# A two-block transformer kernel: gate and up products of 20 tile pairs per FFN layer by a seven-product scheme, with the weight sums as GpSimd additions

## The chip, the core and the metric

The kernel runs on one core of one Trainium2 chip. The metric is the device time of one execution in microseconds (us), lower is better; a median of several runs is compared. Engines are named TensorE (PE, its weight loads PEld), VectorE (DVE), ScalarE (ACT), GpSimd (POOL) and SyncE (SP, which issues the weight loads).

## What is computed

Two models in a row on one sequence of 512 tokens, 1024 wide, all float32: an attention block, then two layers that each end in a gated FFN. The change concerns this function, once per layer, with `D_FF = 2816`:

```python
def gated_conv_ffn(x, w_gate, w_up, conv_w, conv_b, w_down):
    g = jnp.einsum('bsd,df->bsf', x, w_gate)
    g = causal_dwconv3(g, conv_w) + conv_b
    up = jnp.einsum('bsd,df->bsf', x, w_up)
    return jnp.einsum('bsf,fd->bsd', jax.nn.silu(g) * up, w_down)
```

`x` is `rms_norm(h, norm_ffn)`. `causal_dwconv3` is a convolution over the sequence with three taps per channel.

## The kernel before

Every product is made of 128x128 tiles of weights (stationary) and 512 columns of activations (moving), with channels on partitions and tokens in the free dimension. To reach float32 accuracy each operand is split into a high part (a cast to fp32r) and a low part (value less high part), and each tile product is three matmuls (`PASSES`: high-high, high-low, low-high). A unit is one 128-wide output tile of a weight matrix: 8 tiles over the 1024 inputs, 512 KB. SyncE loads a unit into one of two buffers `raw` (`w_load`, two DMAs), ScalarE casts it into one of two buffers `wsp` (`w_hi`, L305), VectorE subtracts (`w_lo`, L321), TensorE runs 24 matmuls (`product`, L364). GpSimd does the low part in other phases (L319). The order on each engine is written out by hand; semaphores that count finished steps are the only link between engines, and each engine works its own queue strictly in order.

In an FFN layer the 2816 hidden channels are 22 tiles, and each tile `f` has a gate unit and an up unit (a tile pair). `pe_ffn` runs them two tiles at a time over banks 0 to 3 of PSUM. `dve_ffn` scales the gate result with the token norm `rbc` (L2441), adds two of the three taps (L2446), multiplies with up (L2456) and makes the low part of the result (L2461); `act_ffn` does the first tap (L2407), SiLU (L2410) and the high part (L2416); `pool_ffn` scales SiLU's result with the norm (L2425). The results `a_r` are the moving operand of the down products (`pe_residual`, units of 8, 8 and 6 tiles, one output tile after the other), which follow at once. `rms_norm`'s factor is made while TensorE does the first FFN products: the sum of squares by a matmul (L1928), root on ScalarE (L1962), reciprocal on VectorE (L1970). It is applied to the products, so the products themselves run on unnormalised activations `u`.

The very last down tile (`pe_last_tile`) is done in halves of 256 columns (L1773). In the odd layer GpSimd multiplies with the gate (L2641) and VectorE makes low parts of what it made (L2645).

## Time and profile before

| | |
|---|---|
| median of 3 runs | 1754.58 us (1753.5 to 1755.64) |
| span of the profiled execution | 1753.3 us |
| TensorE busy | 1722.9 us, 98% |
| its weight loads busy | 1438.5 us, 82% |
| VectorE busy | 955.8 us, 55% |
| ScalarE busy | 776.2 us, 44% |
| GpSimd busy | 406.6 us, 23% |
| read from HBM | 147.02 MB, 85 GB/s |

The device time holds the span and what lies around it. Busy time is the union of an engine's instructions. Matmuls are pipelined: one of 512 columns lasts about 0.39 us from start to end, but the next starts long before that, so the time that a matmul costs is read from a run of them. An instruction's idle time is put down to the engine that released it. The column of a line's name such as L321 is the line in the kernel above.

### The profile page before, as it was taken

To read this page: it belongs to the slowest core of one execution; us is meant where nothing else is said; L and a number is where in the kernel's file an instruction comes from. 1 tells how busy PE (TensorE), PEld (TensorE's weight loads), DVE (VectorE), ACT (ScalarE), POOL (GpSimd) and SP (SyncE) were. 2 spreads that over 40 slices of the span, in tenths; PEclk is the share of its full clock that TensorE was granted. 3 is DMA by queue.
4 is the path that set the end of the run, shared out by engine and by line. 5 is a ranking of instruction groups with operands and counts; after the bars stand their busy time and mean duration, and the time that the engine had idled before them with its cause. 6 is when DMAs were issued, how large, how long until landed. Compare 5 with 4: busy or idle time off the path is not lost.

```text
span 1753.3 us, 25674 instructions
## 1 busy us (share of the span) xinstructions
PE 1722.9 (98%) x8611; PEld 1438.5 (82%) x8611; DVE 955.8 (55%) x1757; ACT 776.2 (44%) x1375; POOL 406.6 (23%) x545
## 2 busy tenths in 40 slices
PE   7999999999999999999999999999999999999998
PEld 7788889999878888888888888888788788888887
DVE  5677867777763334675555555333346555555332
ACT  6666766666652223432443333322364433333222
POOL 4555665655520001000211111011003211111000
PEclk9999999999999999999999999999999999999999
DMA  4112123333323334223233333333232333333332
GB/s 137 52 45 63 42 59 79 81 74 87 75 67 96 96 108 133 61 85 101 84 108 93 94 93 95 120 95 94 96 96 72 87 94 96 96 96 93 93 96 91
DMA packets 284314, 154.42 MB, mean 88 GB/s; under 512 B 12655, under 2 KB 278770, under 8 KB 284242
## 3 DMA queue, kind: packets, MB, share of 16 engines
q1 hardware_dynamic: 281714, 148.69, 29.4%
q0 software_dynamic: 2336, 4.47, 1.1%
q8 instruction: 42, 0.69, 0.2%
q10 hardware_dynamic: 192, 0.33, 0.1%
q14 instruction: 30, 0.25, 0.0%
HBM read 147.02 MB, written 2.16 MB: 85 GB/s over the span
## 4 chain that ended last, share of the span: by engine, by line
PE 82%; DVE 8%; issue 4%; ACT 4%; POOL 1%; DMA 0%; ACTq 0%; DVEq 0%; SPq 0%; POOLq 0%
PE ps L364 65%; PE ps L980 3%; PE ps L2505 2%; PE ps L830 2%; DVE tmp L1323 1%; DVE arena_r L1328 1%; PE ps L843 1%; PE ps L809 1%; ACT tmp L1051 1%; PE ps L788 1%; PE ps L1773 1%; ACT w_split L305 1%; PE ps L347 1%; PE ps L676 1%; DVE tmp L1380 1%
## 5 line engine op out<-in xcount | busy, mean ns | idle before, releaser
L364 PE MATMUL ps<-u,w_split 128*128 128x512 f32 x3705 | 876.9, 394 | 0.0
L364 PEld LDWEIGHTS ps<-u,w_split 128*128 128x128 f32 x3705 | 690.8, 188 | 152.1 <-issue 1.4
L321 DVE TENSOR_TENSOR w_split<-w_raw,w_split 128x1024 fp32r<-128x1024 f32 (+1 forms) x221 | 268.2, 1214 | 434.3 <-ACT w_split L305 434.2
L305 ACT CAST w_split<-w_raw 128x1024 fp32r<-128x1024 f32 (+4 forms) x321 | 289.0, 914 | 412.3 <-PE ps L364 376.6
L364 PE MATMUL ps<-arena_r,w_split 128*128 128x512 f32 x1758 | 402.0, 389 | 1.8 <-POOL w_split L319 1.5
L364 PEld LDWEIGHTS ps<-arena_r,w_split 128*128 128x128 f32 x1758 | 329.5, 188 | 72.2 <-POOL w_split L319 1.9
L2425 POOL TENSOR_TENSOR tmp<-tmp 128x512 f32<-128x512 f32 x44 | 57.1, 1298 | 422.1 <-ACT tmp L2410 422.1
L319 POOL TENSOR_TENSOR w_split<-w_raw,w_split 128x256 fp32r<-128x256 f32 x168 | 122.9, 763 | 23.7 <-ACT w_split L305 23.7
L980 PE MATMUL ps<-u,w_split 128*128 128x264 f32 x768 | 105.8, 287 | 2.0 <-DVE arena_r L1348 1.8
L1921 POOL TENSOR_TENSOR tmp<-tmp 128x512 f32<-128x512 f32 x33 | 46.8, 1417 | 261.1 <-ACT tmp L1877 232.4
L1051 ACT ACTIVATE tmp<-ps,stats 128x144 f32<-128x144 f32 (+3 forms) x128 | 69.4, 542 | 75.1 <-DVE stats L1315 73.0
L980 PEld LDWEIGHTS ps<-u,w_split 128*128 128x128 f32 x768 | 98.6, 188 | 4.6 <-DVE arena_r L1348 2.6
L1918 POOL COPY tmp<-tmp 128x512 f32<-128x512 f32 x5 | 3.2, 649 | 332.3 <-ACT tmp L1877 166.7
L1549 POOL TENSOR_TENSOR tmp<-tmp,ones 128x48 f32<-128x48 f32 x128 | 44.9, 351 | 151.1 <-DVE tmp L1323 151.0
L1315 DVE CUSTOM_DVE_ANT_0 ps<-ps,tmp 128x144 f32<-128x144 f32 (+3 forms) x128 | 65.6, 513 | 23.6 <-issue 22.1
L2410 ACT ACTIVATE tmp<-tmp,vec 128x512 f32<-128x512 f32 x44 | 31.9, 724 | 97.2 <-DVE tmp L2446 97.2
L1067 ACT CAST arena_r<-ps 128x128 fp32r<-128x128 f32 (+3 forms) x128 | 54.6, 426 | 35.1 <-PE ps L809 34.0
L1323 DVE TENSOR_SCALAR tmp<-tmp,stats 128x144 f32<-128x144 f32 (+3 forms) x128 | 66.5, 520 | 4.5
L2446 DVE SCALAR_TENSOR_TENSOR tmp<-tmp,vec 128x512 f32<-128x512 f32 x88 | 65.9, 749 | 5.5 <-DVE tmp L2446 0.3
L2416 ACT CAST arena_r<-tmp 128x512 f32 (+1 forms) x44 | 27.3, 620 | 87.2 <-DVE tmp L2456 87.2
L1328 DVE TENSOR_TENSOR arena_r<-ps,arena_r 128x128 fp32r<-128x128 f32 (+3 forms) x128 | 62.3, 487 | 3.7 <-ACT arena_r L1067 2.2
L809 PE MATMUL ps<-cst,tmp 128*128 128x128 f32 x320 | 57.1, 276 | 3.6 <-DVE arena_r L1328 3.2
(283 smaller groups left out, 1701.1 us busy)
## 6 DMA issues: line engine op xcount, KB each, us to landing
w_raw<-in_w_in_dram SPq DMA_DIRECT2D x118, 256.0 KB, 3.1
w_raw<-in_w_ffn_gate_dram SPq DMA_DIRECT2D x88, 256.0 KB, 3.1
w_raw<-in_w_ffn_up_dram SPq DMA_DIRECT2D x88, 256.0 KB, 3.2
w_raw<-in_w_ffn_down_dram SPq DMA_DIRECT2D x64, 256.0 KB, 3.1
w_raw<-in_w_in_even_dram SPq DMA_DIRECT2D x32, 256.0 KB, 3.0
w_raw<-in_w_in_odd_dram SPq DMA_DIRECT2D x32, 256.0 KB, 3.1
w_raw<-in_w_ffn_down_dram SPq DMA_DIRECT2D x32, 192.0 KB, 2.7
w_raw<-in_w_br_mla_dram SPq DMA_DIRECT2D x16, 256.0 KB, 3.1
```

The costliest lines, as they stand in the source:

```text
L305: ins = act.copy(dst, src)
L319: ins = eng.tensor_tensor(lo[:, at_:at_ + n], r[:, at_:at_ + n], hi[:, at_:at_ + n], ALU.subtract)
L321: ins = eng.tensor_tensor(lo, r, hi, ALU.subtract)
L364: last = pe.matmul(out_ap, w_tile(c, ws, k - n0), moving(k, ms), start=start and n == 0, stop=stop and n == len(total) - 1, skip_group_che ...
L809: ins = pe.transpose(bank(p_bank(b), j * P, (j + 1) * P), prob[:, b % 2, META + j * P:META + (j + 1) * P], ident)
L980: ins = pe.matmul(bank(b, 0, HALF), w_tile(c + j, ws, k), u[:, k, ms, half * HALF:(half + 1) * HALF], start=k == 0 and n == 0, stop=k == K ...
L1051: act.activation(probs(b), scored(b), ACT.Exp, bias=neg[:, b:b + 1], scale=-1.0, accum_out=rs[:, b:b + 1]) \
L1315: dve.tensor_tensor_reduce(out=scored(b), in0=scored(b), in1=mask, scale=1.0, scalar=3.0e38, op0=ALU.add, op1=ALU.min, accum_out=neg[:, b: ...
L1323: dve.tensor_scalar(p, p, ri[:, b:b + 1], None, ALU.mult).then_inc(sem("normed"), 1)
L1328: dve.tensor_tensor(lo, src, hi, ALU.subtract).then_inc(sem("p_split"), 1)
L2425: pool.tensor_tensor(cnv[:, j, :], cnv[:, j, :], rbc[:, 0, :], ALU.mult) \
L2446: dve.scalar_tensor_tensor(out=cnv[:, j, :], in0=gpad[:, j, tap:tap + SEQ], scalar=ffn_vec(layer, tap, f), in1=cnv[:, j, :], op0=ALU.mult, ...
```

## The change

Seen from one tile pair, gate and up are a 2 x 2 block product: two output tiles (gate, up) and two halves of the 1024 inputs on the weight side, and two halves of the inputs and two halves of the 512 tokens on the activation side. Eight block products, in Winograd's form, become seven products `p1` to `p7` of sums of blocks. Each is 4 tiles x 3 passes = 12 matmuls of 256 columns. The first two pairs of each layer (`PLAIN = 2`) stay as they were; 20 pairs use the scheme.

- Weights: a pair is loaded in quarters g1, g2, u1, u2 (the input halves of gate and up, 512 columns wide each, 256 KB). GpSimd makes four sums per pair, in place except the first: e = u1 + u2, u1 += g1, g1 += e, g2 += g1. The seven stationary operands are u1 + g1, g1, g1 + e, e, u2, g2 and g2 + g1. ScalarE casts each (`act_seventh`, L2599 of the changed kernel) and VectorE subtracts (`seventh_low`, L2605), into four slots, three products ahead of TensorE.
- Activations: they must be normalised now, since sums over tokens are formed. VectorE writes `x_tok` (8 instructions, L2636), GpSimd makes four sums 1024 wide (`pool_x`), and ScalarE and VectorE split seven operands `xs` (`act_x`, `dve_x`), once per layer.
- Results: p1 and p6, then p7 and p4 accumulate in one PSUM bank per tile; ScalarE copies it away in between (`snap` 1, 2, 3, L2691), and VectorE adds the right halves and the left half (`add_up_right` L2860, `add_gate_left` L2867, `add_gate_right` L2873). p4 and p3 of a pair are done after p1 of the next pair, the order is p1, p4, p3 (of the pair before), p2, p6, p5, p7. Then the taps (L2697, L2822), SiLU (L2702), product (L2879), high part (L2707) and low part (L2885).
- GpSimd's scaling of SiLU's result is left for the two plain pairs only.
- Semaphores of the prologue are merged, buffers are moved or laid over one another, and the load of `w_spatial` in the odd layer waits for the FFN's last low part.

```diff
+PLAIN = 2
+HT = SEQ // 2
+QUARTER = 4 * P
...
+SEVEN = ("p1", "p4", "p3", "p2", "p6", "p5", "p7")
+OF_LAST = (1, 2)
+ORDER = ([(PLAIN, p) for p in (0, 3, 4, 5, 6)] + [(f, p) for f in range(PLAIN + 1, FT) for p in range(7)]
+         + [(FT, p) for p in OF_LAST])
...
+WEIGHT_OF = {"p1": "g1", "p2": "g2", "p3": "g2", "p4": "u2", "p5": "e", "p6": "g1", "p7": "u1"}
...
-    phase(("ffn", 0), *("full",) * (2 * FT))
+    phase(("ffn", 0), *("full",) * (2 * PLAIN))
...
+            for name in ("u1", "u2", "g1", "g2"):
+                if not first:
+                    if name == "u1":
+                        low_split(sp, layer, i, gs - 2, 6)
+                    elif name != "g2":
+                        low_split(sp, layer, i, gs - 1, 1 if name == "u2" else 2)
...
+            if kind == "p1":
+                out_ = bank(R_BANK + gs % 2, 0, HT)
+                if not (isinstance(i, int) and gs < PLAIN + 2):
+                    pe.wait_ge(sem("ffn_a_done"), per_tile(layer, i, gs, 2))
+            elif kind == "p2":
+                out_ = bank(T_BANK, 0, HT)
+                if not (isinstance(i, int) and gs == PLAIN):
+                    pe.wait_ge(sem("combined"), combined(layer, i, gs - 1, "gate_left"))
+            elif kind == "p5":
+                out_ = bank(Q_BANK, 0, HT)
+                if not (isinstance(i, int) and gs == PLAIN):
+                    pe.wait_ge(sem("combined"), combined(layer, i, gs - 1, "gate_right"))
+            elif kind in ("p4", "p3"):
+                out_ = bank(R_BANK + gs % 2, 0, HT) if kind == "p4" else bank(Q_BANK, 0, HT)
+                pe.wait_ge(sem("combined"), combined(layer, i, gs, "up_right"))
+            else:
+                out_ = bank(R_BANK + gs % 2, 0, HT)
+                pe.wait_ge(sem("snap"), snapped(layer, i, gs, {"p6": 1, "p7": 2}[kind]))
+            for kk in range(4):
+                for n, (ws, ms) in enumerate(PASSES):
+                    ins = pe.matmul(out_, split_slot(layer, fs, pos, ws)[:, kk * P:(kk + 1) * P], XS[kind][:, kk, ms, :],
+                                    start=kind in ("p1", "p2", "p5") and kk == 0 and n == 0, stop=kk == 3 and n == 2,
...
+            act.copy(split_slot(layer, fs, pos, HI), quarter(layer, gs, WEIGHT_OF[kind])).then_inc(sem("s_hi"), 1)
...
+        def seventh_low(eng, layer, i, fs, pos):
+
+            eng.wait_ge(sem("s_hi"), used(layer, i, fs, pos))
+            src = quarter(layer, pair_of(fs, pos), WEIGHT_OF[SEVEN[pos]])
+            eng.tensor_tensor(split_slot(layer, fs, pos, LO), src, split_slot(layer, fs, pos, HI), ALU.subtract) \
+                .then_inc(sem("s_lo_pool" if pos in POOL_LO else "s_lo"), 1)
...
+        def pool_x(pool, layer, m):
+
+            pool.wait_ge(sem("x_dve"), X_STEPS * layer + KT)
+            if m in (1, 3):
+                pool.wait_ge(sem("x_sum"), 4 * layer + m)
+            dst, in0, in1, op = ((T1N, B11, B12, ALU.subtract), (T2, T1N, B22, ALU.add), (T3, B22, B12, ALU.subtract),
+                                 (T4, T2, B21, ALU.subtract))[m]
+            pool.tensor_tensor(dst, in0, in1, op).then_inc(sem("x_sum"), 1)
...
+            def first_sum(i, gs):
+                loaded(pool, layer, i, gs)
+                if not (isinstance(i, int) and gs < PLAIN + 2):
+                    low_split(pool, layer, i, gs - 2, 5)
+                    pool.wait_ge(sem("summed_w"), summed_to(layer, i, gs - 2, 2))
...
+                pool.tensor_tensor(quarter(layer, gs, "e"), quarter(layer, gs, "u1"), quarter(layer, gs, "u2"), ALU.add) \
+                    .then_inc(sem("summed_w"), 1)
...
+            def third_sum(i, gs):
+                pool.wait_ge(sem("summed_w"), summed_to(layer, i, gs, 1))
+                dst = quarter(layer, gs, "u1")
+                pool.tensor_tensor(dst, dst, quarter(layer, gs, "g1"), ALU.add).then_inc(sem("summed_w"), 1)
...
+            def second_sum(i, gs):
+                low_split(pool, layer, i, gs, 0)
+                pool.wait_ge(sem("summed_w"), summed_to(layer, i, gs, 3))
+                dst = quarter(layer, gs, "g1")
+                pool.tensor_tensor(dst, dst, quarter(layer, gs, "e"), ALU.add).then_inc(sem("summed_w"), 1)
...
+            def fourth_sum(i, gs):
+                low_split(pool, layer, i, gs, 3)
+                pool.wait_ge(sem("summed_w"), summed_to(layer, i, gs, 2))
+                dst = quarter(layer, gs, "g2")
+                pool.tensor_tensor(dst, dst, quarter(layer, gs, "g1"), ALU.add).then_inc(sem("summed_w"), 1)
...
+            def period(i, fs):
+                if fs == FT:
+                    return
+                fourth_sum(i, fs)
+                if fs < FT - 1:
+                    first_sum(i, fs + 1)
+                    third_sum(i, fs + 1)
+                    second_sum(i, fs + 1)
+
...
+            plain_gate(0)
+            w_lo(dve, c0 + 2)
+            dve_x_token(dve, layer, range(0, 4))
+            taps(0, 0, cnv[:, 0, :])
+            dve_x_token(dve, layer, range(4, KT))
+            w_lo(dve, c0 + 3)
+            plain_hidden(0)
+            dve_x(dve, layer, "p1")
+            plain_low(0)
+            dve_x(dve, layer, "p2")
+            plain_gate(1)
+            taps(0, 1, cnv[:, 1, :])
+            seventh_low(dve, layer, 0, *ORDER[0])
+            dve_x(dve, layer, "p6")
+            seventh_low(dve, layer, 0, *ORDER[1])
+            dve_x(dve, layer, "p5")
+            dve_x(dve, layer, "p7")
+            seventh_low(dve, layer, 0, *ORDER[2])
...
+            def add_up_right(i, gs):
+                dve.wait_ge(sem("snap"), snapped(layer, i, gs, 3))
+                dve.tensor_tensor(bank(R_BANK + gs % 2, HT, SEQ), bank(Q_BANK, 0, HT), up2[:, gs % 2, :], ALU.add) \
+                    .then_inc(sem("combined"), 1)
...
+            def add_gate_right(i, gs):
+                dve.wait_ge(sem("snap"), snapped(layer, i, gs, 2))
+                dve.wait_ge(sem("s_used"), used(layer, i, gs + 1, 2))
+                right = gpad[:, gs % 2, 2 + HT:2 + SEQ]
+                dve.tensor_tensor(right, bank(Q_BANK, 0, HT), right, ALU.add).then_inc(sem("combined"), 1)
...
+            def hidden(i, gs):
+                dve.wait_ge(sem("ffn_silu"), per_tile(layer, i, gs))
+                dve.wait_ge(sem("s_used"), used(layer, i, gs + 1, 1))
+                dve.wait_ge(sem("combined"), combined(layer, i, gs, "up_right"))
+                dve.scalar_tensor_tensor(out=bank(CONV_BANK + gs % 2), in0=bank(R_BANK + gs % 2), scalar=-1.0,
+                                         in1=cnv[:, gs % 2, :], op0=ALU.mult, op1=ALU.mult).then_inc(sem("ffn_a_done"), 1)
...
+            def period(i, fs):
+                begun, carried = fs < FT, fs > PLAIN
+                if carried:
+                    add_up_right(i, fs - 1)
+                if fs == FT:
+                    w_lo(dve, c0 + 2 * PLAIN)
+                if begun:
+                    lo_ahead(i, fs, 0)
+                    if not carried:
+                        plain_hidden(1)
+                        plain_low(1)
+                        dve_x(dve, layer, "p4")
+                if carried and begun:
+                    lo_ahead(i, fs, 1)
+                if carried and fs > PLAIN + 1:
+                    hidden_low(i, fs - 2)
+                if carried and begun:
+                    lo_ahead(i, fs, 2)
+                if carried:
+                    add_gate_right(i, fs - 1)
+                if begun:
+                    lo_ahead(i, fs, 3)
+                    if not carried:
+                        dve_x(dve, layer, "p3")
+                if carried:
+                    taps(i, fs - 1, bank(CONV_BANK + (fs - 1) % 2))
+                if fs == FT:
+                    w_lo(dve, c0 + 2 * PLAIN + 1)
+                if begun:
+                    add_gate_left(i, fs)
+                    lo_ahead(i, fs, 4)
+                    lo_ahead(i, fs, 5)
+                if carried:
+                    hidden(i, fs - 1)
+                if begun:
+                    lo_ahead(i, fs, 6)
+                if fs == FT:
+                    hidden_low(i, FT - 1)
+
+            periods(dve, period)
 
 
```

VectorE's queue for one tile pair before, in the last pair of the second layer (`ps` is PSUM, `tmp` holds gate, taps and product):

```order
L2441 TENSOR_TENSOR tmp<-ps,tmp 128x512 [waits ffn_conv,w_used]
L321 TENSOR_TENSOR w_split<-w_raw,w_split 128x1024 [waits w_hi]
L2446 SCALAR_TENSOR_TENSOR tmp<-tmp,vec 128x512 [waits ffn_tap]
L2446 SCALAR_TENSOR_TENSOR tmp<-tmp,vec 128x512 [waits ffn_conv]
L321 TENSOR_TENSOR w_split<-w_raw,w_split 128x1024 [waits w_hi]
L2456 TENSOR_TENSOR tmp<-ps,tmp 128x512 [waits ffn_a_lo,w_used,ffn_scaled]
L2461 TENSOR_TENSOR arena_r<-tmp,arena_r 128x512 [waits ffn_a_hi]
```

Two instructions of 1024 columns for the weights, five of 512 for the tile's result.

VectorE's queue for one period of the changed kernel, one of those behind the loop of 4 x 4 periods, from behind `add_up_right` (L2860) to the last low part (`w_raw_b`, `w_raw` and `e_sum` hold the quarters and sums):

```order
L2605 TENSOR_TENSOR w_split<-w_raw_b,w_split 128x512 [waits s_hi] x2
L2885 TENSOR_TENSOR arena_r<-ps,arena_r 128x512 [waits ffn_a_hi]
L2605 TENSOR_TENSOR w_split<-e_sum,w_split 128x512 [waits s_hi]
L2873 TENSOR_TENSOR tmp<-ps,tmp 128x256 [waits s_used,snap]
L2605 TENSOR_TENSOR w_split<-w_raw_b,w_split 128x512 [waits s_hi]
L2822 SCALAR_TENSOR_TENSOR ps<-tmp,vec,ps 128x512 [waits ffn_tap]
L2822 SCALAR_TENSOR_TENSOR ps<-tmp,vec,ps 128x512 [waits ffn_conv]
L2867 TENSOR_TENSOR tmp<-ps,tmp 128x256 [waits s_used,snap]
L2605 TENSOR_TENSOR w_split<-w_raw,w_split 128x512 [waits s_hi]
L2605 TENSOR_TENSOR w_split<-w_raw_b,w_split 128x512 [waits s_hi]
L2879 SCALAR_TENSOR_TENSOR ps<-ps,tmp 128x512 [waits combined,s_used,ffn_silu]
L2605 TENSOR_TENSOR w_split<-w_raw_b,w_split 128x512 [waits s_hi]
```

Seven low parts of 512 columns stand where two of 1024 stood, three additions of 256 are new (the third one heads the period), and the product with SiLU stands behind the low parts of the fifth and sixth place.

ScalarE's queue in the same period of the changed kernel, from behind `snap` 3 of the pair before (L2691) to the high part of that pair's result:

```order
L2599 CAST w_split<-w_raw_b 128x512 [waits s_used,pair_load0]
L2691 COPY tmp<-ps 128x256 [waits s_used,ffn_conv]
L2599 CAST w_split<-w_raw_b 128x512 [waits s_used,summed_w]
L2599 CAST w_split<-e_sum 128x512 [waits s_used,summed_w]
L2599 CAST w_split<-w_raw_b 128x512 [waits s_used,summed_w]
L2697 ACTIVATE ps<-tmp,vec 128x512 [waits ffn_a_lo,combined]
L2599 CAST w_split<-w_raw 128x512 [waits s_used,pair_load1]
L2691 COPY tmp<-ps 128x256 [waits s_used,ffn_conv]
L2702 ACTIVATE tmp<-ps,vec 128x512 [waits ffn_conv]
L2599 CAST w_split<-w_raw_b 128x512 [waits s_used,pair_load0]
L2599 CAST w_split<-w_raw_b 128x512 [waits s_used,summed_w]
L2707 CAST arena_r<-ps 128x512 [waits ffn_a_done]
```

Seven casts, three copies out of PSUM (the third is `snap` 3 ahead of these rows), the first tap, SiLU and the high part of the result, which now stands ahead of the next period's `snap` 3.

## Rows read from the trace of the kernel before

**Rows 1.** The page, busy times and the chain that ended last

```profile
PE 1722.9 (98%) x8611; PEld 1438.5 (82%) x8611; DVE 955.8 (55%) x1757; ACT 776.2 (44%) x1375; POOL 406.6 (23%) x545
...
PE 82%; DVE 8%; issue 4%; ACT 4%; POOL 1%; DMA 0%; ACTq 0%; DVEq 0%; SPq 0%; POOLq 0%
```

**Rows 2.** Stretch table: layer 0, second gate/up product to the down products

```profile
core 0: us, PE busy (x) PEld busy (x) DVE busy (x) ACT busy (x) POOL busy (x), PEclk, DMA share, GB/s
870.13:1107.91 237.78, 237.78 (x1035) 194.19 (x1034) 129.66 (x153) 89.69 (x110) 27.89 (x22) 1.00 0.32 94
```

**Rows 3.** Groups of instructions, 900 to 1050 us: busy us, mean ns | idle before

```profile
L364 PE MATMUL ps<-u,w_split 128*128 128x512 f32 x654 | 150.6, 393 | 0.0
...
L321 DVE TENSOR_TENSOR w_split<-w_raw,w_split 128x1024 fp32r<-128x1024 f32 x28 | 34.3, 1226 | 44.1 <-ACT w_split L305 44.1
```

**Rows 4.** Chain that ended last, last tile, 256-column matmuls: start us, us, what

```profile
1728.26 3.14 PE ps L1773 x24
...
1734.59 6.21 PE ps L1773 x51
...
1741.62 2.87 PE ps L1773 x24
```

**Rows 5.** Groups by shape, ScalarE, whole span

```profile
L2410 ACT ACTIVATE tmp<-tmp,vec 128x512 f32<-128x512 f32 x44 | 31.9, 724 | 97.2 <-DVE tmp L2446 97.2
...
L1067 ACT CAST arena_r<-ps 128x256 fp32r<-128x256 f32 x32 | 11.9, 373 | 11.7 <-PE ps L809 11.7
...
L305 ACT CAST w_split<-w_raw 128x512 fp32r<-128x512 f32 x1 | 0.6, 622 | 4.5 <-PE ps L364 4.5
```

**Rows 6.** Groups by shape, VectorE; then two taps in the timeline

```profile
L2456 DVE TENSOR_TENSOR tmp<-ps,tmp 128x512 f32<-128x512 f32 x44 | 30.1, 684 | 0.0
...
L2727 DVE TENSOR_TENSOR big<-ps,big 128x256 f32<-128x256 f32 x2 | 0.8, 424 | 9.5 <-PE ps L1773 9.5
...
L321 DVE TENSOR_TENSOR w_split<-w_raw,w_split 128x512 fp32r<-128x512 f32 x1 | 0.7, 693 | 0.0
...
961.43 1.64 DVE L2446 SCALAR_TENSOR_TENSOR tmp<-tmp,vec 128x512 f32<-128x512 f32 x2
```

**Rows 7.** Groups by shape, GpSimd, 512 and 1024 wide

```profile
L2425 POOL TENSOR_TENSOR tmp<-tmp 128x512 f32<-128x512 f32 x44 | 57.1, 1298 | 422.1 <-ACT tmp L2410 422.1
...
L321 POOL TENSOR_TENSOR w_split<-w_raw,w_split 128x1024 fp32r<-128x1024 f32 x5 | 12.3, 2468 | 17.2 <-ACT w_split L305 17.2
```

**Rows 8.** Timeline, GpSimd and VectorE in the odd layer: start us, us, instruction

```profile
1324.53 2.97 POOL L2641 TENSOR_TENSOR tmp<-tmp,big 128x512 f32<-128x512 f32 x2
...
1325.26 1.10 DVE L2645 TENSOR_TENSOR arena_r<-tmp,arena_r 128x512 fp32r<-128x512 f32 x1 [0.73 <-ACT arena_r L2582]
...
1326.28 0.74 DVE L2626 SCALAR_TENSOR_TENSOR tmp<-ps,vec,tmp 128x512 f32<-128x512 f32 x1
...
1334.25 1.74 POOL L2641 TENSOR_TENSOR tmp<-tmp,big 128x512 f32<-128x512 f32 x1
...
1334.98 1.56 DVE L2645 TENSOR_TENSOR arena_r<-tmp,arena_r 128x512 fp32r<-128x512 f32 x1
```

**Rows 9.** Timeline at the end of a down product's unit

```profile
1725.02 3.03 PE L1773 MATMUL ps<-arena_r,w_split 128*128 128x256 f32 x24
1725.30 1.05 ACT L305 CAST w_split<-w_raw 128x1024 fp32r<-128x1024 f32 x1 [3.03 <-PE ps L364]
1726.38 1.23 DVE L321 TENSOR_TENSOR w_split<-w_raw,w_split 128x1024 fp32r<-128x1024 f32 x1 [2.85 <-ACT w_split L305]
```

**Rows 10.** Timeline, start of the FFN of layer 0

```profile
871.37 3.35 DVE L1970 RECIPROCAL tmp<-tmp 128x512 f32<-128x512 f32 x1 [3.00 <-ACT tmp L1962]
874.77 0.68 DVE L2441 TENSOR_TENSOR tmp<-ps,tmp 128x512 f32<-128x512 f32 x1
...
881.58 18.80 PE L364 MATMUL ps<-u,w_split 128*128 128x512 f32 x81
```

**Rows 11.** DMA issues: KB each, median us from issue to landing

```profile
w_raw<-in_w_ffn_gate_dram SPq DMA_DIRECT2D x88, 256.0 KB, 3.1
```

552 lines of the change are left out of this document (392 added, 160 removed).

## The prediction

> **What bounds the kernel now.** I read the page's busy times and chain first. TensorE is busy for 98% of the span, and 82% of the chain that ended last lies on it [rows 1]: a reader sees a kernel that only gets faster if TensorE has less to do, and nothing else becomes later than TensorE. Next, the stretch of the first layer's gate and up products, from the second product to the first one of the down projection: 237.8 us, TensorE busy throughout, VectorE 129.7, ScalarE 89.7, GpSimd 27.9, clock 1.00 [rows 2]. In its steady part 654 matmuls of 512 columns take 150.6 us [rows 3], 0.230 us each, so a tile pair (48 of them) costs 11.05 us. VectorE's splitting there idled 44.1 us until ScalarE's, so it has slack.
>
> **TensorE's own saving.** A pair changes from 48 matmuls of 512 columns to 7 x 12 = 84 of 256. The nearest rows are the last tile's 256-column matmuls, also with a fresh weight tile each: 24 in 2.87 to 3.14 us, 51 in 6.21 [rows 4], so 0.120 to 0.131; I take 0.120, the undisturbed run. A product is 1.44 us and a pair 84 x 0.120 = 10.08 us instead of 11.05. So a scheme that drops one product in eight can save at most 0.97 us (9%) a pair, since a narrow matmul costs more than half of a wide one. For 0.131 it would be nothing.
>
> **What the other engines get.** Per pair ScalarE issues 7 high parts of 512 columns (0.62), three PSUM copies of 256 (0.37), tap and SiLU (0.72 each) and one cast: about 7.5 us [rows 5]. VectorE issues 7 low parts (0.69), three additions of 256 (0.42), two taps (1.64 together), the product and its low part (0.69 each): about 9.1 us, or 8.1 because a queued instruction starts 0.08 before the one ahead of it ends [rows 6, 8]. GpSimd issues 4 sums of 1.30 [rows 7]: 5.2. Each is under 10.08, so busy times alone promise a gain. Two things take it away.
>
> The first is **a port**. In the odd layer's gate an addition of GpSimd ran from 1324.53 to about 1325.8; a VectorE subtraction with both inputs in SBUF issued at 1325.26 took 1.10 us instead of 0.69. One issued at 1334.98, with GpSimd at work from 1334.25 to 1335.99, took 1.56. Both are 0.69 plus what was left of GpSimd's instruction less 0.14. GpSimd instructions issued during these took 1.74, not 1.30. L2626, with PSUM as one input, kept 0.74 [rows 8]. All seven low parts have two SBUF inputs, and GpSimd's sums read SBUF. The Trainium skill (SBUF — State Buffer, the single rule) calls the shared port an exclusive lock under which the loser fully blocks; with the whole remainder instead of the remainder less 0.14, two hits a pair would add 0.28 us a period, some 11 us in all.
>
> The second is **latency round a loop**. A ScalarE cast starts 0.28 us after TensorE has begun the next product, VectorE 0.03 after ScalarE's end [rows 9].
>
> **One period, by hand.** Zero is the end of the copy of up's right half (`snap` 3) of the tile before. VectorE's `add_up_right` 0.04 to 0.46; TensorE starts p4 at 0.50 and is through p3 at 3.38, seen by VectorE at 3.62. Meanwhile low parts: p2's 0.60 to 1.29; GpSimd's fourth sum from 1.35 to 2.64, which holds p6's (issued 1.48) until 3.17; `hidden_low` to 3.78; p5's 3.70 to 4.39. `add_gate_right` 4.31 to 4.73. ScalarE's first tap 4.77 to 5.49. But p7's low part, issued at 4.65, is ahead of the taps in VectorE's queue, and GpSimd's first sum, which had to wait for loads (issued behind the last low part of the period before, 3.1 us to land [rows 11]) and then for p5's part, has run since 4.25: p7's part ends at 6.09. Taps 6.01 to 7.65. SiLU 7.69 to 8.39, and ScalarE's next cast (p4's) 8.33 to 8.95. Behind the taps VectorE did `add_gate_left` and p1's low part by 8.60, which releases GpSimd's last sum, 8.66 to 9.95. So p4's low part, issued 8.99, always meets it and ends at 10.50. `hidden` 10.42 to 11.12, ScalarE's `hidden_hi` 11.16 to 11.75, and the next `snap` 3, behind it in the queue, 11.69 to 12.07. **A period is 12.07 us**: TensorE works 10.08 and waits 2.0 in front of p4, because p1 alone (1.44 us) covers the way from p7 over ScalarE and VectorE. If GpSimd's first sum starts just before p5's low part rather than behind it (the loads may land at 3.4 and the part is issued at 3.70), that part is held too and the period is 12.9. Without any holding it is 10.7. These are the bounds.
>
> **The start of each FFN.** Zero is 870.13, the second plain product; the reciprocal ends at 4.6 and the fourth plain product could start at 11.45 [rows 10]. VectorE now has this before that product's weights are split: scaling to 5.3; the third product's low part, held 0.54 by GpSimd's first sum, to 7.0; four `x_tok` (0.67 apart, two SBUF inputs), held 1.0 by the next sum, to 10.8; taps to 12.3; four more, held 0.9 by GpSimd's scaling, to 16.1; the low part, 17.2. TensorE waits 5.8 us. Then, one after the other: product 17.8, ScalarE's two casts 19.4, x of p1 20.7 (GpSimd's second `pool_x` is issued behind the first, and gets the port at 20.65 for 2.47 [rows 7]), the plain low part 23.6, x of p2 24.8, scaling 25.3, first tap 26.05, taps 27.7, p1's low part 28.3: p1 starts there. GpSimd goes on with a weight sum (held, to 30.7), the scaling (32.4, both with holds of VectorE's), the third `pool_x` 33.4 to 35.9 and the fourth 35.95 to 38.4. ScalarE casts the third result by 37.0; VectorE's x of p7, issued 37.05, is held to 38.3 and ends at 39.4, and p6's low part, behind it in the queue, at 40.0. So p6 starts at 40.1. Two parts, the plain tile's product and its low part, x of p4 and p3, an addition and the next p1's part add 6.9: the second pair's p1 starts at **47.0**, where TensorE alone would need 16.97 + 5 x 1.44 = 24.2. My bounds are 30 (these steps mostly hidden) and 52.
>
> **The end.** Behind the last pair p4 and p3 have no p1 as cover: 1.2 + 2.9 = 4.1 us to the down product, whose first unit is split by 3.0 and whose later ones have cover. The loads of W_spatial, the merged semaphores and the moved buffers I cost at nothing: TensorE does not wait for them in the same stretches now, and the work in front of them is longer.
>
> **Sum.** 47.0 + 19 x 12.07 + 4.1 = 280.4 us in place of 237.8 [rows 2], so +42.6 a layer and +85.2 for two. The profiled execution spans 1753.3 us and the median is 1754.6; 1.3 lies around it. The forecast is 1754.6 + 85.2 = **1840 us**, 4.9% slower.
>
> **Rivals.**
> *A third hold* (p5's low part): 47.0 + 19 x 12.9 + 4.1 = 296.2, +58.4 a layer: 1871. For it: 3.4 against 3.7 is close. Against: the loads may share queues and land later.
> *Holds rare, only the loop's latency*: 39 + 19 x 10.7 + 4.1 = 246.4, +8.6 a layer: 1772. For it: order decides who is held, and a period may settle where parts and sums miss each other. Against: the last sum is released by p1's part and p4's comes right behind.
> *TensorE stays the bound, faster*: the loop hides under 10.08. With a start of 30, 30 + 191.5 + 4.1 = 225.6, -12.2 a layer: 1730. It decides at (237.8 - 4.1 - start) / 19: with my start the period would have to be under 9.8, which even TensorE's own 10.08 excludes, so the start has to be under 42 as well. For it: every busy time is under 10.08. The Trainium skill (TensorE: Matmul & The Clock Gate, back-to-back issue gap) gives N/2.4 + 2.5 ns, an estimate of 109 ns at 256 columns and of 9.2 us a pair; by it this rival would be 30 + 19 x 9.2 + 4.1 = 208.9, or 1697. The measured 0.230 and 0.120 [rows 3, 4] lie 6 and 10% above the formula, so I don't use it.
> *It doesn't cut TensorE's work*: at 0.131 a matmul a pair is 11.0 us; with the start's waits still +15 to +25 a layer, slower also.
>
> **Chances.** Forecast 0.42, third hold 0.2, latency only 0.23 (slower in nearly all of it), TensorE bound 0.13, near nothing 0.02. A measurement of this kernel tells 0.2% (3.5 us) from no change. Slower 0.85, same 0.02, faster 0.13. The range leaves out the faster case and little of the third hold: 1765 to 1880.
>
> **What would show it.** Matmuls of 256 columns at 0.120 in a run. TensorE idle some 2 us a pair, all in front of p4, released by VectorE's addition of `up_right`. Low parts with a mean near 1.06 instead of 0.69, and values of 1.4 to 1.7 where GpSimd is at work. Waits of 10 us and more in all among the first products of each FFN. A period under 10.5, or TensorE still 98% busy, would make me wrong; so would low parts of 0.69 throughout, with the period still 12 (then latencies that I don't see).

## The result and the profile after

The changed kernel takes **1879.6 us** (1875.5 to 1885.7) where the kernel before took 1755.1 on the same chip: a ratio of 1.071 (95% interval 1.069 to 1.073). It is 7.1% slower, 124.5 us. The runs below come from several chips, on which the kernel before took 1755.1 to 1757.5, so that differences of 1 to 3 us between runs of different chips are read from the ratios. One of the four runs of e4 took 8967 us for a reason that the record doesn't show, and is left out of its ratio (the others: 1793.7 to 1796.2).

The page of the changed kernel, busy times and TensorE's granted clock in 40 slices:

```profile
PE 1739.4 (93%) x10051; PEld 1525.9 (81%) x10051; DVE 1190.7 (63%) x2067; ACT 899.7 (48%) x1709; POOL 608.2 (32%) x673
...
PEclk9999999999999999999899889999999798999999
```

TensorE, busy for 98% before [rows 1], is now busy for 93%, and the clock row has dents. They lie where the FFNs are. The stretch table of the first layer's FFN (second plain product to the first down product), and two single periods of it:

```profile
869.73:1172.12 302.39, 246.86 (x1755) 238.05 (x1753) 245.07 (x305) 150.12 (x275) 129.67 (x86) 0.90 0.25 73
...
957.36:971.16 13.80, 11.78 (x86) 11.58 (x85) 11.11 (x14) 6.83 (x15) 5.46 (x4) 0.88 0.27 78
932.89:945.15 12.26, 10.39 (x87) 10.19 (x86) 10.61 (x15) 6.83 (x15) 5.49 (x4) 1.00 0.30 86
```

The stretch that took 237.8 us [rows 2] takes 302.4: +64.6 us. The second layer's takes 300.6 (1445.57 to 1746.19), so the two account for the loss. A period (from one third copy, L2691, to the next) has no single length: 14 of the 38 take under 12.35 us, 20 take 13.7 on average, 4 lie between; the mean is 12.97. The two rows show what differs: the granted clock.

TensorE in the timeline, a short period and then a long one (start, us, what, idle before):

```profile
932.42 1.70 PE L2552 MATMUL ps<-xs_u,w_split 128*128 128x256 f32 x12 [0.95 <-DVE ps L2879]
933.96 1.59 PE L2552 MATMUL ps<-xs_b,w_split 128*128 128x256 f32 x12
935.39 1.59 PE L2552 MATMUL ps<-xs_t,w_split 128*128 128x256 f32 x12
936.81 4.48 PE L2552 MATMUL ps<-xs_u,w_split 128*128 128x256 f32 x36
941.12 1.59 PE L2552 MATMUL ps<-xs_b,w_split 128*128 128x256 f32 x12
944.58 1.69 PE L2552 MATMUL ps<-xs_u,w_split 128*128 128x256 f32 x12 [1.87 <-DVE ps L2879]
...
1007.94 2.18 PE L2552 MATMUL ps<-xs_u,w_split 128*128 128x256 f32 x12 [1.86 <-DVE ps L2879]
1009.91 2.64 PE L2552 MATMUL ps<-xs_b,w_split 128*128 128x256 f32 x12
1012.40 1.58 PE L2552 MATMUL ps<-xs_t,w_split 128*128 128x256 f32 x12
1013.82 4.46 PE L2552 MATMUL ps<-xs_u,w_split 128*128 128x256 f32 x36
```

And the granted clock (the figure third from the end) in two stretches of the long period's p1:

```profile
1008.40:1008.60 0.20, 0.20 (x4) 0.20 (x3) 0.07 (x1) 0.20 (x2) 0.00 (x0) 1.00 0.10 28
1009.00:1009.40 0.40, 0.40 (x4) 0.40 (x3) 0.33 (x1) 0.38 (x1) 0.00 (x0) 0.50 0.87 264
```

In the first period, products follow each other by 1.43 to 1.44 us, and p2, p6 and p5 take 941.12 - 936.81 = 4.31 for 36: 0.120 a matmul, the size that was taken from [rows 4]. In the second, p1 takes 1.97 us and p4 2.49, which for p4 is 0.207 a matmul. p1 begins at full clock (1.00 until 1008.6); by 1009.0 the granted clock is 0.50, the level of 1.2 GHz, and it is back at 1.00 when p3 runs. TensorE's idle time stands in front of p1 and not, as forecast, in front of p4, and what ends it is VectorE's hidden product (L2879).

VectorE and GpSimd in the same short period:

```profile
935.09 1.44 DVE L2605 TENSOR_TENSOR w_split<-w_raw_b,w_split 128x512 fp32r<-128x512 f32 x1 [0.58 <-ACT w_split L2599]
...
937.98 1.45 DVE L2605 TENSOR_TENSOR w_split<-w_raw_b,w_split 128x512 fp32r<-128x512 f32 x1
...
942.39 1.53 DVE L2605 TENSOR_TENSOR w_split<-w_raw_b,w_split 128x512 fp32r<-128x512 f32 x1 [0.45 <-ACT w_split L2599]
943.84 0.69 DVE L2879 SCALAR_TENSOR_TENSOR ps<-ps,tmp 128x512 f32<-128x512 f32 x1
```

```profile
934.68 1.29 POOL L2786 TENSOR_TENSOR w_raw_b<-w_raw_b 128x512 f32<-128x512 f32 x1 [3.47 <-DVE w_split L2605]
937.57 1.31 POOL L2768 TENSOR_TENSOR e_sum<-w_raw 128x512 f32<-128x512 f32 x1 [1.59 <-DMA w_raw<-in_w_ffn_gate_dram]
...
942.10 1.27 POOL L2780 TENSOR_TENSOR w_raw<-w_raw,e_sum 128x512 f32<-128x512 f32 x1 [1.51 <-DVE w_split L2605]
```

These are the three holds of the working: p6's, p7's and p4's low parts. The rule (0.69, plus what is left of GpSimd's instruction, less 0.14) gives 1.43, 1.45 and 1.53 for them, against 1.44, 1.45 and 1.53 in the rows. The product of the tile is queued behind the last one. Between 921 and 1168 us no wait of ScalarE or VectorE is ended by GpSimd: ScalarE's are ended by TensorE and VectorE, VectorE's nearly all by ScalarE. So the sums cost by their holds here, and not because somebody waits for their results.

The start of the FFN, TensorE and below it ScalarE ahead of p6:

```profile
886.76 8.55 PE L409 MATMUL ps<-arena_r,w_split 128*128 128x512 f32 x24 [5.54 <-DVE w_split L366]
897.67 1.70 PE L2552 MATMUL ps<-xs_u,w_split 128*128 128x256 f32 x12 [2.36 <-DVE w_split L2605]
900.49 1.69 PE L2552 MATMUL ps<-xs_u,w_split 128*128 128x256 f32 x12 [1.12 <-DVE w_split L2605]
914.39 5.46 PE L2552 MATMUL ps<-xs_u,w_split 128*128 128x256 f32 x24 [12.21 <-ACT tmp L2691]
...
921.29 1.60 PE L2552 MATMUL ps<-xs_u,w_split 128*128 128x256 f32 x12
```

```profile
912.41 0.62 ACT L2669 CAST arena_r<-tmp 128x512 fp32r<-128x512 f32 x1 [5.43 <-DVE tmp L2833]
...
913.88 0.36 ACT L2691 COPY tmp<-ps 128x256 f32<-128x256 f32 x1
```

Counted from 869.73, the fourth plain product starts at 17.0 (forecast 17.2), p1 at 27.9 (28.3), p6 at 44.7 (40.1), the second pair's p1 at 51.6 (47.0).

### The profile page after: what moved, and what is told of

Same layout as the page of the kernel before. It is cut to its first block and busy times, and to the rows that moved or that the text cites. A ratio compares the mean times of both kernels' runs of the same rounds, so it can differ in the third digit from the quotient of the medians.

```text
span 1879.5 us, 30474 instructions
## 1 busy us (share of the span) xinstructions
PE 1739.4 (93%) x10051; PEld 1525.9 (81%) x10051; DVE 1190.7 (63%) x2067; ACT 899.7 (48%) x1709; POOL 608.2 (32%) x673
## 5 line engine op out<-in xcount | busy, mean ns | idle before, releaser
L409 PE MATMUL ps<-arena_r,w_split 128*128 128x512 f32 x1902 | 441.2, 393 | 12.8 <-DVE w_split L366 11.1
L409 PE MATMUL ps<-u,w_split 128*128 128x512 f32 x1641 | 400.7, 396 | 0.0
L366 DVE TENSOR_TENSOR w_split<-w_raw,w_split 128x1024 fp32r<-128x1024 f32 x141 | 170.7, 1210 | 297.6 <-ACT w_split L350 297.6
L2552 PE MATMUL ps<-xs_u,w_split 128*128 128x256 f32 x1920 | 269.0, 300 | 95.9 <-DVE ps L2879 64.5
L409 PEld LDWEIGHTS ps<-u,w_split 128*128 128x128 f32 x1641 | 304.3, 189 | 63.2 <-issue 0.5
L350 ACT CAST w_split<-w_raw 128x1024 fp32r<-128x1024 f32 (+4 forms) x241 | 204.8, 868 | 300.4 <-PE ps L409 264.8
L2552 PEld LDWEIGHTS ps<-xs_u,w_split 128*128 128x128 f32 x1920 | 254.7, 206 | 104.7 <-DVE ps L2879 64.4
L2552 PE MATMUL ps<-xs_b,w_split 128*128 128x256 f32 x960 | 147.8, 311 | 3.2 <-DVE ps L2860 3.2
L2552 PEld LDWEIGHTS ps<-xs_b,w_split 128*128 128x128 f32 x960 | 142.0, 222 | 3.8 <-issue 3.6
L2605 DVE TENSOR_TENSOR w_split<-w_raw_b,w_split 128x512 fp32r<-128x512 f32 x120 | 122.8, 1024 | 29.3 <-ACT w_split L2599 27.7
L2605 DVE TENSOR_TENSOR w_split<-w_raw,w_split 128x512 fp32r<-128x512 f32 x120 | 118.3, 986 | 29.2 <-ACT w_split L2599 27.5
L1025 PEld LDWEIGHTS ps<-u,w_split 128*128 128x128 f32 x768 | 98.6, 188 | 4.6 <-DVE arena_r L1393 2.6
L2599 ACT CAST w_split<-w_raw_b 128x512 fp32r<-128x512 f32 x120 | 72.4, 618 | 17.7 <-PE ps L2552 17.6
L2599 ACT CAST w_split<-w_raw 128x512 fp32r<-128x512 f32 x120 | 72.5, 619 | 16.3 <-PE ps L2552 16.2
```

The source lines that it names most:

```text
L350: ins = act.copy(dst, src)
L366: ins = eng.tensor_tensor(lo, r, hi, ALU.subtract)
L409: last = pe.matmul(out_ap, w_tile(c, ws, k - n0), moving(k, ms), start=start and n == 0, stop=stop and n == len(total) - 1, skip_group_che ...
L1025: ins = pe.matmul(bank(b, 0, HALF), w_tile(c + j, ws, k), u[:, k, ms, half * HALF:(half + 1) * HALF], start=k == 0 and n == 0, stop=k == K ...
L2552: ins = pe.matmul(out_, split_slot(layer, fs, pos, ws)[:, kk * P:(kk + 1) * P], XS[kind][:, kk, ms, :], start=kind in ("p1", "p2", "p5") a ...
L2599: act.copy(split_slot(layer, fs, pos, HI), quarter(layer, gs, WEIGHT_OF[kind])).then_inc(sem("s_hi"), 1)
```

## The experiments

In what follows a part is the low part of a product's weights (L2605), a hold is the time by which an addition of GpSimd lengthens it, and a long period is one of about 13.7 us.

Several theories stood after this reading. **Mine**: the loop over VectorE with its three holds gives 12.26 us, and the long periods are the same loop with TensorE at its lower clock behind its own idle time. **Its rivals**: the long periods are the third hold on the port (p5's part); the bank that p1 waits for makes the period; the holds don't matter, since latency between the engines would take the time anyway.

### TensorE kept at work (e1)

```
+ behind p7: 12 x pe.matmul(bank(0, 0, HT), XS["p1"][:, 0, HI, 0:P], XS["p1"][:, 0, HI, :])
```

> Twelve extra matmuls of 256 columns (XS times XS) go into bank 0, which nothing reads then, behind p7 of each period; the output stays. My theory (the hand schedule is right, 12.26 us a period, and the periods of 13.8 us come from TensorE's clock at its 1.2 GHz level after its idle of 1.5 to 2 us): every period is near 12.3 us, p1 and p4 take 1.44 us each, and the time falls by 2 x 19 x (12.96 - 12.3) = 25 us, to about 1855. Rival A (the long periods are the third hold on the port, and the clock only follows): periods of 12.3 and 13.8 stay, time 1875 to 1885. Rival B (extra work on TensorE is in the way, since p1 starts behind it): slower, 1885 to 1930.

Measured: 1850.4 us, ratio 1.055 (1.053 to 1.056), 29 us less than the change (25 expected). TensorE in the timeline; L2584 are the added matmuls:

```profile
1002.14 1.59 PE L2552 MATMUL ps<-xs_b,w_split 128*128 128x256 f32 x12
1003.57 1.58 PE L2584 MATMUL ps<-xs_u 128*128 128x256 f32 x12
1005.67 1.69 PE L2552 MATMUL ps<-xs_u,w_split 128*128 128x256 f32 x12 [0.52 <-DVE ps L2883]
1007.21 1.66 PE L2552 MATMUL ps<-xs_b,w_split 128*128 128x256 f32 x12
1008.71 1.59 PE L2552 MATMUL ps<-xs_t,w_split 128*128 128x256 f32 x12
```

All the steady periods are now 12.2 to 12.5 us (11.9 for the last full one), and p1 and p4 take 1.5 us. Adding work made the kernel faster, by what 20 long periods were longer: 20 x (13.72 - 12.26) = 29. The clock's share is settled, and the first rival falls: p5's part takes 0.67 us throughout the steady part of e1, with GpSimd's sums as they were. It is held in long periods because p1 and p4 are late, not the other way round.

### Sums without holds (e2)

```
-   pool.tensor_tensor(dst, dst, quarter(layer, gs, "g1"), ALU.add)
+   pool.tensor_tensor(dst[:, 0:1], dst[:, 0:1], quarter(layer, gs, "g1")[:, 0:1], ALU.add)
...
```

> GpSimd's four weight sums of a pair are made on one column of 512 in place of all (in the first layer the first sum of the first two pairs stays whole); five of seven products so use weights that are not summed. Every wait stays. My theory (the holds on the port are in the loop: p4's low part always, p7's too): low parts take 0.69 us, the period is 10.7 to 11.0 us, and with shorter gaps TensorE's clock stays up more; 2 x 19 x (12.96 - 10.9) = 78 us less, plus a few us at the start: about 1795 (1780 to 1815). Rival (the loop is latency between engines, and a held part would have waited anyway): 1860 to 1880.

Most products then use weights that are not summed, so this kernel leaves out a part of the computation.

Measured: 1779.9 us, ratio 1.014 (1.013 to 1.016): 100 us less than the change, at the lower end of what I expected. VectorE's low parts in groups, 960 to 1084 us:

```profile
L2605 DVE TENSOR_TENSOR w_split<-w_raw,w_split 128x512 fp32r<-128x512 f32 x36 | 24.8, 690 | 7.0 <-ACT w_split L2599 6.5
L2605 DVE TENSOR_TENSOR w_split<-w_raw_b,w_split 128x512 fp32r<-128x512 f32 x35 | 24.1, 689 | 6.8 <-ACT w_split L2599 6.3
L2605 DVE TENSOR_TENSOR w_split<-e_sum,w_split 128x512 fp32r<-128x512 f32 x12 | 8.3, 690 | 0.0
```

All parts take 0.69 us, the period is 10.5 us everywhere, and the clock is 1.00 in the steady part. TensorE's waits in front of p1 are down to 0.15 to 0.24 us and its clock doesn't fall there, so removing the holds also removes the clock's loss: of the 100 us, 38 x (12.97 - 10.51) = 93 are the period, the rest is the start (the first third copy comes at 48.4 us behind the second plain product, 51.8 in the change).

### Four banks (e3)

```
-   R_BANK = 4                                    bank(R_BANK + gs % 2)
+   R_BANKS = (0, 1, 4, 5)                        bank(R_BANKS[gs % 4])
-   pe.wait_ge(sem("ffn_a_done"), per_tile(layer, i, gs, 2))
+   pe.wait_ge(sem("ffn_a_done"), per_tile(layer, i, gs, 4))
```

> The up and right sums of the products get four PSUM banks (0, 1, 4, 5) in place of two, and p1 waits for the hidden product of four tiles back, not two; work and order stay. My theory (that wait only shows a loop which would close in front of p4 anyway, 0.2 us later): TensorE's wait moves from p1 to p4, the period is 12.1 at full clock and the clock falls as before; -5 to -10 us, about 1872. Rival (the shared bank is what stretches the period over TensorE's own 10.1): 1790 to 1830.

Measured: 1850.0 us (1843.5 to 1858.0), ratio 1.053 (1.051 to 1.055), 30 us less. TensorE:

```profile
1004.64 1.58 PE L2552 MATMUL ps<-xs_u,w_split 128*128 128x256 f32 x12
1007.97 1.66 PE L2552 MATMUL ps<-xs_b,w_split 128*128 128x256 f32 x12 [1.74 <-DVE ps L2860]
...
1020.21 2.36 PE L2552 MATMUL ps<-xs_b,w_split 128*128 128x256 f32 x12 [1.99 <-DVE ps L2860]
```

The mechanism is as I expected: the wait stands in front of p4 and is ended by the addition of up's right half, as in the prediction, and the steady periods at full clock are 11.85 to 12.15, two of 12.24 and 10.48 aside (12.07 by hand). The rival (1790 to 1830) falls. The size is not: I had -5 to -10 us. The profiled runs are 23 us apart: 8 by the bank (38 x 0.2), 13 since 11 periods are long in place of 20 (9 x 1.5), and two intermediate ones fewer. The gaps are a little shorter here: in steady periods at full clock 1.58 to 1.80 us (once 1.91), 1.75 to 1.99 where the clock was lost, against 1.81 to 2.13 where it was lost in the change. That this is why it falls less often is likely, but not shown, since the two groups overlap; the spread of this kernel's runs, 14 us, fits a number of long periods that changes from run to run.

### The hidden product first (e4)

```
+   hidden(i, fs - 1)
    lo_ahead(i, fs, 5)          # p4's low part
-   hidden(i, fs - 1)
```

> In VectorE's queue the hidden product stands ahead of p4's low part instead of behind it; all else stays. My theory (p4's low part is held 0.8 us by GpSimd's last sum, and the loop closes over the hidden product behind it): the product is done 1.5 us earlier, the period is 10.7 to 11.2 us, 2 x 19 x 1.8 = 68 us less, about 1812 (1800 to 1835). Rival A (the hold then delays p4's low part so that TensorE waits for it instead): period near 12, 1850 to 1870. Rival B (SiLU on ScalarE is late, and the product can't go earlier): 1870 to 1885.

Measured: 1795.3 us, ratio 1.022 (1.020 to 1.024), 84 us less than the change (68 expected), so both rivals fall. The one edit moves p4's low part behind the product. VectorE (first p7's part, then the product, and p4's and p3's parts together) and TensorE:

```profile
1002.88 0.69 DVE L2605 TENSOR_TENSOR w_split<-w_raw_b,w_split 128x512 fp32r<-128x512 f32 x1 [0.16 <-ACT w_split L2599]
...
1006.57 0.68 DVE L2879 SCALAR_TENSOR_TENSOR ps<-ps,tmp 128x512 f32<-128x512 f32 x1
1007.17 2.08 DVE L2605 TENSOR_TENSOR w_split<-w_raw_b,w_split 128x512 fp32r<-128x512 f32 x2
1009.17 0.42 DVE L2860 TENSOR_TENSOR ps<-ps,up_right 128x256 f32<-128x256 f32 x1
```

```profile
1007.75 1.58 PE L2552 MATMUL ps<-xs_u,w_split 128*128 128x256 f32 x12
1009.73 1.67 PE L2552 MATMUL ps<-xs_b,w_split 128*128 128x256 f32 x12 [0.39 <-DVE ps L2860]
```

The period is 10.63 us at a clock of 1.00. p4's part is still held by 0.8 us, but no longer ahead of the product, and TensorE waits 0.4 us in place of 1.9. The edit isn't clean, though: the engines now meet at other times. p7's part is not held any more (0.69), p6's by 0.2 us at most, p1's by 0.4, so the holds of a period fall from 2.35 us to about 1.2, and p4's unheld 0.6 us leaves the loop as well. e4 shows that the order of two lines decides the loop; how much of the 84 us is the place of one hold it doesn't tell.

### The addition first as well (e5), x sums on VectorE (e6)

```
    add_up_right(i, fs - 1)
+   lo_ahead(i, fs - 1, 6)      # e5: p3's low part, from the period before
```

```
-   pool_x(pool, layer, m)
+   pool_x(dve, layer, m)       # e6: the four sums of x, behind p1's low part of x
```

> As e4 (the hidden product ahead of p4's low part), and besides VectorE's addition of up's right half goes ahead of p3's low part. In e4 the period was 10.63 us, with 0.39 us in which TensorE waits in front of p4 for that addition, which stands behind two low parts that took 2.08 us together (held by GpSimd's last sum). My theory (that is the last stretch of the loop that lies open): TensorE is the bound, a period is 84 x 0.120 = 10.1 us, 2 x 19 x 0.5 = 19 us less than e4: 1776 (1770 to 1785). Rival (VectorE with its holds is the bound, 9.1 to 10.5 us of work a period): 1790 to 1800, and TensorE waits for a low part.

> As e4, and the four sums of x (128x1024 each) are made by VectorE behind p1's low part of x, not by GpSimd. The steady part is e4's. My theory (GpSimd's sums hold VectorE's port in the start, and are slower than VectorE's own: 2.36 to 3.34 us each against 1.22): VectorE pays 4.9 us and gets back some 6 us of holds and 4 us of waiting for the last sum; the start falls by 4 to 7 us a layer, time 1782 to 1788. Rival (the start is bound by the order in VectorE's queue, whoever makes the sums): 1793 to 1803.

Measured: e5 1785.1 us, ratio 1.016 (1.014 to 1.018), at the upper edge of my range and under the rival's; e6 1792.5 us, ratio 1.020 (1.018 to 1.022), a miss, 3 us less than e4 (4 by the ratios) where I had 7 to 13. In e5 the periods vary from 10.0 to 10.8 (one 11.2). That e6 gains so little speaks for its rival, whose time it has within 1 us. e6's start, TensorE, where the second plain product begins at 873.37:

```profile
917.22 5.28 PE L2552 MATMUL ps<-xs_u,w_split 128*128 128x256 f32 x24 [7.91 <-ACT tmp L2691]
```

p6 starts at 43.9 (44.7 in the change), still behind ScalarE's first copy. So it isn't the maker of the x sums that sets the start. On ScalarE that copy is queued behind the high part of the second plain tile (L2669) and the x of p4, and the high part waits 7.8 us in e6, 5.4 in the change, for VectorE's hidden product of that tile, which stands behind other parts in VectorE's queue.

### The start in another order (e7, e8), banks again (e9)

```
  VectorE's queue behind the first plain gate and the third product's low part ("x p1": part of x; "p1": of a weight)
-   x_tok 0..3; taps 0; x_tok 4..7; 4th low part; hidden 0; x p1; low 0; x p2; gate 1; taps 1; p1; x p6; p2; x p5; x p7; p6; p5; ...
+   4th low part; x_tok 0..7; taps 0; p1; x p1; T1N; T2; x p2; p2; x p6; p6; hidden 0; p5; x p5; T3; low 0; p7; x p7; gate 1; ...
  ScalarE's, from p6's high part
-   p6; p5; hi 1; x p4; copy 1; ...
+   p6; copy 1; p5; x p5; hi 0; p7; copy 2; x p7; p1'; tap 1; x p4; ...
```

> As e5, and the start of each FFN is ordered anew: VectorE makes the sums of x; the fourth plain product's split stands ahead of the token sums; p1's, p2's and p6's parts stand ahead of the plain tiles' hidden products; the first copy of a product's result stands ahead of the x of p4 on ScalarE. All values are still computed. By hand: p1 starts at 18 to 19, p6 at 25, p1 of the second pair at 32 (51.6 before); with some holds of GpSimd's weight sums, and as TensorE is then short of work for p4 (about 5 us later than p1), the start is worth 10 to 13 us a layer. My theory: 1776 - 23 = 1753 (1745 to 1765), at the kernel before or just under it. Rival (VectorE's sum of work in the start is the bound, order gives nothing): 1770 to 1780.

> The changed kernel with e7's start alone; the steady part is as in the change. My theory (start, period and end add up, as in the sum of the prediction): 1880 - 23 = 1857 (1850 to 1865). Rival (the first periods are bound by what the start has put off, and give it back): 1868 to 1880.

> As e7, and the up and right sums have four PSUM banks as in e3. In e7 the periods were 9.9 to 10.7 us (mean 10.5), with TensorE waiting 0.2 to 0.3 us in front of p1 for the hidden product that still reads the shared bank, and 0.24 us in front of p4. My theory (TensorE at 10.1 us a pair is the bound once both are gone; p4's wait shrinks since VectorE's queue is no longer tied to p1): periods 10.1 to 10.3, 7 to 14 us less than e7's 1773: 1763 (1758 to 1768). Rival (VectorE, busy for about 10 us a period with its holds, is the bound): 1770 to 1775.

Measured: e7 1773.3 us, ratio 1.010 (1.008 to 1.011), 12 less than e5, in the rival's range and not in mine; e8 1865.8 us, ratio 1.061 (1.058 to 1.064), 14 less than the change, just above my range; e9 1774.8 us, ratio 1.011 (1.009 to 1.012), no different from e7, which is the rival's time. e8's start, where zero is 868.93:

```profile
892.90 5.75 PE L2552 MATMUL ps<-xs_u,w_split 128*128 128x256 f32 x24 [4.41 <-DVE w_split L2605]
...
904.65 1.68 PE L2552 MATMUL ps<-xs_u,w_split 128*128 128x256 f32 x12
914.51 0.77 PE L2552 MATMUL ps<-xs_b,w_split 128*128 128x256 f32 x2 [8.19 <-DVE ps L2859]
```

The second pair's p1 starts at 35.7 instead of 51.6, and 8.2 us of that is given back in front of the first p4, for work that was put off. So a start that is 16 us shorter is worth 6 to 7 us a layer (e7 against e5, e8 against the change): less than my 10 to 13, and more than the rival's nothing. e9 tells what e5's periods are: with the bank's wait gone the mean stays at 10.5, and the wait is back in front of p4. The stretch table of e9, 960 to 1084 us, and VectorE in one of its periods:

```profile
960.00:1084.00 124.00, 121.36 (x1000) 119.56 (x1000) 116.94 (x167) 82.39 (x156) 66.56 (x48) 1.00 0.34 99
```

```profile
1006.07 1.54 DVE L2605 TENSOR_TENSOR w_split<-w_raw_b,w_split 128x512 fp32r<-128x512 f32 x1
...
1008.14 1.47 DVE L2605 TENSOR_TENSOR w_split<-w_raw,w_split 128x512 fp32r<-128x512 f32 x1
```

VectorE, busy for 55% of the FFN before (129.7 of 237.8 [rows 2]), is busy for 94% of this stretch, two of its parts held by 0.8 us each. That VectorE's queue, filled up by holds, is now what keeps the period at 10.5 us is my reading of it; e11 and e12 try it.

### The last two: hold moved (e11), holds gone (e12), with e10 as their base

```
  e10:  ScalarE: ..., x p4, p4's cast, copy 3, SiLU 1, p3's cast, x p3, hi 1
        VectorE: ..., p4's part, add_up_right, p3's part, x p3, hidden 1, low 1
  e11:  e10, and   add_up_right(i, fs - 1); lo_ahead(i, fs - 1, 5); lo_ahead(i, fs - 1, 6)
  e12:  e10, with e2's sums of one column
```

> As e9, and in the first pair of each FFN ScalarE's third copy and VectorE's addition behind it, and the parts of p3, stand ahead of the second plain tile's SiLU, casts and hidden product. In e7 TensorE stood still for 7.6 us in front of the first p4, for these. My theory (p4 can start 4 us earlier, and 2 to 3.5 us of it stay, as VectorE still has the plain tile's work): 4 to 7 us less than e9: 1757 (1752 to 1762), level with the kernel before or behind it by up to 0.3%. Rival (the plain tile's work then delays the second pair by as much): as e9.

> As e10, and in the steady part ScalarE's third copy stands ahead of its cast of the hidden product, and p4's low part stands behind VectorE's addition of up's right half, so that it runs when GpSimd's last sum is over. In e9 and e10 VectorE is busy for 95% of the steady part, 2.2 us of a period by holds of p1's and p4's parts. My theory (VectorE's queue with its holds is what keeps the period at 10.5): without p4's hold 10.3 to 10.4 us, 4 to 8 us less than e10: 1764 (1761 to 1768). Rival (p4 is now last behind copy, addition and its own part, and the hold moves to another part): 1768 to 1780.

> As e10, with GpSimd's weight sums made on one column of 512 as in e2, so that most products use weights that are not summed. My theory: with neither holds nor the shared bank TensorE is the bound and a period 10.1 us; 0.43 x 36 = 15 us less, and some 3 us a layer less in the start: 1750 (1744 to 1756), level with the kernel before. So even sums that cost VectorE nothing would leave no gain, since start and end spend what TensorE saves. Rival (only the steady part keeps it from the gain): under 1740. Rival (VectorE's own work is the bound even unheld): 1762 to 1770.

Measured: e10 1770.9 us, ratio 1.008 (1.007 to 1.010); e11 1771.5 us, ratio 1.009 (1.007 to 1.010); e12 **1741.7 us, ratio 0.992 (0.991 to 0.994)**. The first FFN's stretch and the steady part in e12, and below them the first FFN's in e10:

```profile
870.11:1101.79 231.68, 220.84 (x1755) 215.97 (x1754) 196.65 (x309) 151.62 (x275) 27.62 (x82) 0.99 0.33 95
...
960.00:1084.00 124.00, 124.00 (x1042) 124.00 (x1041) 103.19 (x174) 85.51 (x160) 11.07 (x51) 1.00 0.36 106
```

```profile
869.53:1116.03 246.50, 227.13 (x1755) 218.97 (x1753) 232.22 (x309) 150.95 (x275) 118.97 (x82) 0.98 0.31 89
```

e10 is 4 us under e9, the least that I expected of it, though above the 1752 to 1762 that I had counted from a faster e9: its first third copy comes 5.4 us earlier (38.3 us behind the second plain product, 43.7 in e9), and 3.1 of it are given back in the first period, 15.9 us instead of 12.8. In e11 the hold of p4's part is gone (0.69 us), and most periods lie between 10.36 and 10.5, but their mean is e10's, 10.5, and so is the time: the rival, p4 behind copy, addition and part. e11's stretch from 960 to 1084 us:

```profile
960.00:1084.00 124.00, 122.11 (x1000) 119.69 (x999) 112.52 (x167) 82.41 (x155) 64.99 (x48) 1.00 0.34 99
```

VectorE is busy for 91% of it, 95% in e10 (117.78 us), with the same period. So the share that VectorE is busy doesn't set the period by itself, and what does in e11 stays open. In e12, which like e2 leaves out most of the summing, TensorE is busy throughout and a period is 10.02 us, 84 x 0.119, 1.03 less than the 11.05 of a pair before [rows 3]. Of the 21 us that this makes for 20 pairs the start and the end take back 15: the FFN takes 231.7 us against 237.8 [rows 2]. I had 1750, as I put the start's holds at 3 us a layer. The price of summing on GpSimd, in e10's order, is the difference of the two stretches, 246.5 - 231.7 = 14.8 us a layer: 18 periods x 0.45 = 8, and 6.7 up to the second pair's third copy.

No version that computes everything beats the kernel before; e10 comes to within 0.8%. Sums made in a way that leaves VectorE's port alone (while the weights are loaded, for instance) weren't tried. If they cost nothing at all, e12 tells what they would bring in this order: 0.8%.

## Why the prediction was right, and where its sum was short

The forecast of slower was right, and 1879.6 us is at the upper edge of the range (1880). That it lies inside is luck: two of the four runs took 1881.2 and 1885.7. The forecast itself, +85 us, was 39 us short of +124.5. The way to slower was as forecast: a loop over VectorE, lengthened by holds on the port.

- **A matmul of 256 columns at 0.120**: right, 0.120 in the change and 0.119 in e12. The formula of the Trainium skill (TensorE: Matmul & The Clock Gate, back-to-back issue gap), which gives an estimate of 0.109, was rightly left out; that section gives it for an isolated matmul, and the runs decide. The measured 0.230 for 512 columns is 7% above it, not 6.
- **The port**: right. Three parts a period are held at the forecast places and take 1.44, 1.45 and 1.53 us (1.69, 1.44 and 1.51 by hand). e2 and e12 take the sums away, and with nobody waiting for the sums' results in the change's steady part, what went with them is the holds. The Trainium skill (SBUF — State Buffer, the single rule) calls the shared port an exclusive lock, and the trace agrees that the later instruction is put off. Full remainders would give 1.57, 1.59 and 1.67, so the measured 0.14 less decides. The prediction's 11 us for that difference counted two holds a period where its own schedule has three.
- **The period**: 12.07 by hand. At full clock it is 12.26 in the change and 11.85 to 12.15 in e3. The 0.2 us is a step that I missed: p1 writes the bank that the hidden product of two tiles back reads. So p1 waits, and no longer covers the way over ScalarE and VectorE. It moved the idle time from p4 to p1, and costs 19 x 0.2 = 4 us a layer.
- **The mis-sized term** is "TensorE works 10.08": it took every product at full clock. In 20 of 38 periods the end of p1 and all of p4 ran at 1.2 GHz's level, 1.45 us more each period, 29 us in all (e1), of 39 that were missing. The prediction priced idle time as time alone.
- **The third hold** (1871) gave nearly the measured time by the wrong mechanism. p5's part is held in long periods (1.66 us), but these holds vanish in e1 (0.67), where GpSimd's sums are untouched.
- **The start**: 51.6 instead of 47.0. Right to 0.4 us as far as p1, at 27.9. Then a queue was misread: p6 doesn't start with its own part (ready at 40.4, forecast 40.0) but with ScalarE's first copy, and that is queued behind the second plain tile's high part and the x of p4. The high part waits 5.4 us for VectorE's hidden product, behind p6's and p5's parts, which are held to 1.75 us each. So p6 starts at 44.7, not 40.1, and the second pair 4.6 us late in this layer, 3.5 in the other. The end was right (4.6 against 4.1).
- **What would show it wrong**: low parts near 1.06 (measured 0.99 to 1.02, and 1.20 for those of e_sum) and waits of 10 us and more in the start (12.2) came as said. The place of the wait, "all in front of p4", did not.

In the two FFNs 42 us are missing, 22.0 and 20.2 (302.4 and 300.6 against 280.4); together they take 127.4 us more than twice the 237.8. The profiled execution as a whole is 126.2 us longer than before's, so the rest of the program takes back 1, and the other 2 lie between that execution and the medians. The period's mean, 12.97 instead of 12.07, makes 38 x 0.9 = 34 of the 42, the two starts 8, and the ends next to nothing. Of the 34 the clock has 29 and the bank 8, less what the first and last periods of a layer (11.4 to 11.7, and 10.5) lie under 12.26, plus the four intermediate ones.
